# Two weight blocks split ahead of four projections, the ring's loads moved on SyncE's queue, squares added in pairs on GpSimd

## What is computed

```python
for i in range(4):
    h = adaln(x, norm_g[i, 0], shift[:, 0], scale[:, 0])
    x = x + 0.5 * gate[:, 0, None] * swiglu(h, ffn_w_in[i, 0], ffn_w_out[i, 0])
    h = adaln(x, norm_g[i, 1], shift[:, 1], scale[:, 1])
    y = (rwkv7_time_mix, mamba2_ssd_mix, swa_sink_attention)[i % 3](h, ...)
    x = x + gate[:, 1, None] * y
    h = adaln(x, norm_g[i, 2], shift[:, 2], scale[:, 2])
    x = x + 0.5 * gate[:, 2, None] * swiglu(h, ffn_w_in[i, 1], ffn_w_out[i, 1])
# rms_norm(x, g) = x * rsqrt(mean(x * x over features) + eps) * g
# adaln(x, g, shift, scale) = rms_norm(x, g) * (1 + scale) + shift
```

## Time and profile before

| | |
|---|---|
| Median of 3 runs | 3921.24 us (3918.16 to 3923.84) |
| The profiled execution's own time | 3914.14 us |
| Its span, first to last instruction | 3912.5 us |
| Busy: PE / DVE / ACT / POOL | 88% / 60% / 39% / 4% |
| Instructions on PE / DVE / ACT / POOL | 28885 / 3355 / 2038 / 148 |
| Mean granted TensorE clock | 0.905 |
| HBM read | 669 MB, 172 GB/s over the span |

### The profile page before, as it was taken

The page is one execution under the profiler, slowest core; times in us unless marked ns, Lnnn a source line. Parts: engine busy times, 40 slices in busy tenths (PEclk is TensorE's granted clock), DMA queues, the critical chain, the costliest instruction groups (busy, mean ns, idle before and its releaser), DMA issues. The chain is left out here.

```text
span 3912.5 us, 68263 instructions
## 1 busy us (share of the span) xinstructions
PE 3438.6 (88%) x28885; PEld 3248.8 (83%) x28885; DVE 2347.7 (60%) x3355; ACT 1507.4 (39%) x2038; POOL 155.0 (4%) x148
## 2 busy tenths in 40 slices
PE   6688999999985788999997499999599999859799
PEld 5578999999983778999995499999389998648599
DVE  5547886456764436767676557676657646354454
ACT  3314444434452114444462244444454444311243
POOL 0001111110000100000000000000000000001000
PEclk9769999998997888999996699999799999878799
DMA  8326885445831004768541047685037444200142
GB/s 338 130 119 245 314 311 228 182 187 225 313 135 54 2 2 180 299 235 310 213 172 46 1 186 297 231 310 202 35 153 297 188 185 159 77 21 2 75 175 84
DMA packets 74781, 676.76 MB, mean 173 GB/s; under 512 B 8480, under 2 KB 12608, under 8 KB 52160
## 3 DMA queue, kind: packets, MB, share of 16 engines
q1 hardware_dynamic: 30400, 509.96, 33.6%
q10 hardware_dynamic: 41472, 151.01, 10.1%
q0 software_dynamic: 2688, 12.59, 1.2%
HBM read 669.29 MB, written 4.23 MB: 172 GB/s over the span
## 5 line engine op out<-in xcount | busy, mean ns | idle before, releaser
L1109 DVE TENSOR_TENSOR w_split<-ring,w_split 128x1024 fp32r<-128x1024 f32 x705 | 873.5, 1242 | 603.5 <-ACT w_split L1004 601.1
L1004 ACT ACTIVATE w_split<-ring 128x1024 fp32r<-128x1024 f32 x705 | 742.8, 1057 | 1077.2 <-PE banks L934 853.5
L932 PE MATMUL banks<-u_split,w_split 128*128 128x256 f32 x3840 | 1093.1, 285 | 13.9 <-DVE w_split L1109 7.3
L933 PE MATMUL banks<-u_split,w_split 128*128 128x256 f32 x3840 | 1090.1, 284 | 0.0
L934 PE MATMUL banks<-u_split,w_split 128*128 128x256 f32 x3840 | 1089.9, 284 | 0.0
L932 PEld LDWEIGHTS banks<-u_split,w_split 128*128 128x128 f32 x3840 | 741.5, 193 | 19.8 <-DVE w_split L1109 16.2
L933 PEld LDWEIGHTS banks<-u_split,w_split 128*128 128x128 f32 x3840 | 741.2, 193 | 0.5
L934 PEld LDWEIGHTS banks<-u_split,w_split 128*128 128x128 f32 x3840 | 740.7, 193 | 0.0
L932 PE MATMUL banks<-h_split,w_split 128*128 128x256 f32 x1920 | 543.6, 283 | 2.9 <-DVE w_split L1109 2.9
L933 PE MATMUL banks<-h_split,w_split 128*128 128x256 f32 x1920 | 543.4, 283 | 0.0
L934 PE MATMUL banks<-h_split,w_split 128*128 128x256 f32 x1920 | 543.3, 283 | 0.0
(11 more groups left out here) (395 smaller groups left out, 3986.8 us busy)
## 6 DMA issues: line engine op xcount, KB each, us to landing
ring<-stream SPq DMA_DIRECT2D x147, 3072.0 KB, 10.8
bufs<-ada ACTq DMA_DIRECT2D x288, 512.0 KB, 10.9
bufs<-ada SPq DMA_DIRECT2D x8, 2048.0 KB, 9.0
bufs<-ada POOLq DMA_DIRECT2D x8, 1024.0 KB, 7.6
bufs<-c_rows SPq DMA_DIRECT2D x8, 512.0 KB, 4.3
bufs<-gate_rows POOLq DMA_DIRECT2D x32, 128.0 KB, 8.0
ring<-stream SPq DMA_DIRECT2D x3, 1024.0 KB, 4.9
ring<-stream SPq DMA_DIRECT2D x1, 2816.0 KB, 10.4
```

Source lines behind the costliest of these rows:

```text
L932: pe.matmul(out, w(0), x(0), start=start, stop=False, skip_group_check=True)
L933: pe.matmul(out, w(0), x(1), start=False, stop=False, skip_group_check=True)
L1004: nc.scalar.activation(w_split[:, slot, 0, :], piece(j, b), ACT.Copy).then_inc(high.sem, 1)
L1109: e = nc.vector.tensor_tensor(w_split[:, slot, 1, :], piece(j, b), w_split[:, slot, 0, :].bitcast(F32), ALU.subtract)
```

## The change

It has three parts.

1. *First blocks split ahead.* The first dense unit of each layer gets `ahead`: two keys (the first two blocks of the mixer's first projection, `r0`, `mb_in`, `sw_qk`, `r1`) and two slots. At its end ScalarE copies both high parts behind the unit's last ones, and VectorE writes the first low part ahead of the residuals and the second behind them. `core.split_early` is 2 in the next stage, so that `weight_high` and `weight_low` do nothing for those two blocks, and the waits count from there. The window projection takes its slots from buffer 8 in place of 7, and its band mask moves.
2. *Ring ahead of the stores.* In `first_ada_stage` unit 0 is issued ahead of the fourth ada slice, units 1 and 2 right behind it, and the two stores of bias rows come after them.
3. *Pairs.* `pair_sums` on GpSimd adds squares 2q and 2q+1; `token_sums` takes four chunks in place of eight. It is used in three centering stages, the norm behind the last of them, seven dense units and four output stages.

```diff
@@ first_ada_stage, SyncE
             for k in range(FIRST_HALVES):
                 if k >= 3:
+                    core.load_ahead(sync, None, 1)
                     sync.wait_ge(step.sem, step.at(4 * (k - 2)))
                 sync.dma_start(slots[k % 3], core.ada[k, :, :]).then_inc(loaded[k % 3].sem, loaded[k % 3].count(16))
+            core.load_ahead(sync, None, SLOTS - 1)
             for q in range(2):
                 sync.wait_ge(copied.sem, copied.at(4 * q + 4))
...
-            core.load_ahead(sync, None, SLOTS - 1)
             sync.wait_ge(stored.sem, stored.at(32))
@@ weight_high, weight_low (the first line), project_first_pair (the last two)
+    if b < core.split_early:
+        return
...
-    pe.wait_ge(low.sem, low.at(2))
+    if core.split_early < 2:
+        pe.wait_ge(low.sem, low.at(2))
@@ new
+def pair_sums(core, pool, squares, squared, paired, per=1, offset=0):
+
+    for q in range(KC // 2):
+        pool.wait_ge(squared.sem, squared.at((2 * q + 2) // per + offset))
+        pool.tensor_tensor(squares[:, 2 * q, :], squares[:, 2 * q, :], squares[:, 2 * q + 1, :], ALU.add)\
+            .then_inc(paired.sem, paired.count(1))
@@ NextNorm.on_tensor (center_stage alike)
-            token_sums(core, pe, self.squares, self.bank, self.squared, self.summed)
+            token_sums(core, pe, self.squares[:, 0:KC:2, :], self.bank, self.paired, self.summed, n=KC // 2)
@@ glu_stage, ScalarE
+            if ahead:
+                act.wait_ge(h_low.sem, h_low.at(n))
+                for key, slot in zip(*ahead):
+                    unit, at, size, _ = core.place[key]
+                    act.wait_ge(core.loaded[unit % SLOTS].sem, 16 * (unit // SLOTS + 1))
+                    act.activation(slot, core.ring[:, unit % SLOTS, at:at + size], ACT.Copy).then_inc(high.sem, 1)
+                high.made += len(ahead[0])
@@ glu_stage, VectorE
+            if ahead:
+                ahead_low(0)
             for c in range(KC):
...
+            if ahead:
+                ahead_low(1)
+                low.made += len(ahead[0])
             if after:
                 after.on_vector(dve)
@@ layer
-    layer_ffn(core, i, 0, early=2 if i else 0)
+    first = ("r0", "mb_in", "sw_qk", "r1")[i]
+    layer_ffn(core, i, 0, early=2 if i else 0, ahead=([(first, 0), (first, 1)], core.weight_slots(8)[0:2]))
```

More of the change, by code:

```diff
@@ L490, in project_split @@
     w = weight_parts(core, b, key, slots, kcs)
-    pe.wait_ge(low.sem, low.at(b + 1))
+    if b >= core.split_early:
+        pe.wait_ge(low.sem, low.at(b + 1 - core.split_early))
     for k in range(kcs):
@@ L797, in _ @@
                 root_of_tokens(core, act, turn=1)
+        @block.gpsimd
+        def _(pool):
+            pair_sums(core, pool, squares, squared, center_paired, per=2)
+            if after:
+                after.on_gpsimd(pool)
         @block.vector
@@ L845, in pair_norm_stage, with glu_stage @@
     core.end_stage()
-def glu_stage(core, key, n, src, residual, gates=None, ada=None, shift=None, early=0, pre=None, then=None, next_key=None):
+def glu_stage(core, key, n, src, residual, gates=None, ada=None, shift=None, early=0, pre=None, then=None, next_key=None, ahead=None):
     nc = core.nc
@@ L1101, in _ @@
                 gated.made += n
+        if gates is None and after:
+            @block.gpsimd
+            def _(pool):
+                after.on_gpsimd(pool)
         @block.vector
@@ L1201, in next_low, with ahead_low @@
                                         w_split[:, b, 0, :].bitcast(F32), ALU.subtract).then_inc(low.sem, 1)
+            def ahead_low(b):
+                key, slot = ahead[0][b], ahead[1][b]
+                unit, at, size, _ = core.place[key]
+                dve.wait_ge(high.sem, high.at(6 * n + b + 1))
+                nc.vector.tensor_tensor(core.ring_split[unit % SLOTS][:, at:at + size], core.ring[:, unit % SLOTS, at:at + size],
+                                        slot.bitcast(F32), ALU.subtract).then_inc(low.sem, 1)
             link = chain(core, dve, "dve")
@@ L1226, in glu_stage @@
     core.end_stage()
+    core.split_early = len(ahead[0]) if ahead else 0
 def log1p_series(dve, link, out, e, t, z):
```

23 lines of the change are left out of this document (16 added, 7 removed).

## The result

The changed kernel takes 3894.39 us against 3922.46 of the kernel before (medians of four runs each); the ratio is 0.9929, with a 95% interval of 0.9913 to 0.9945: 28 us or 0.7% less, 21.6 to 34 by the interval. One of the four, at 7354 us, was disturbed: it is left out of the ratio but counts in the median, which lies between 3888.38 and 3900.39. The forecast was 23.7 us less, 3897.5, and 3884 to 3913 for its range. The same kernel was timed twice more, with a ratio of 0.9924 (0.9908 to 0.9940) and one of 0.9945 (0.9930 to 0.9959), so the three give 21 to 30 us.

The account below looks back on a forecast made before the run. TensorE was busy for 88% of the span, so only seams between stages could shorten: 12.8 us (split blocks) + 16.5 (pairs) - 5.6 (load order) = 23.7 less than the median 3921.24, giving 3897.5 us; range 3884 to 3913.

Parts of the forecast that it names:

- The window wait: Window projection's start: TensorE no longer waits for a weight block's low part and starts 4.4 us earlier.
- The sign against it: Window stage: if the second product pair starts less than 3 us earlier, the split-block forecast is wrong.
- The byte count: Start, SyncE's queue: 11.5 MB take 26.8 us at 430 GB/s, then two stores of 2.1 MB take 4.9, until 60.9.
- a queue served in order: SyncE's queue at the start: stores issued behind the weight units land after them; next stage starts 13.6 us later.
- the rest of that stage keeps its distances: Stage after the stores: beyond the 7.99 us wait saved, nothing else shifts, so the net is 5.6 us lost.
- Rival A: Start: stores land beside the weight units, not held up; the load order gains 8.0 us, total 3883.9; chance 0.10.
- three centering stages: Sums in centering: TensorE's rows halve from 6.99 us, first add delays 0.7; gain 2.8 each, 8.4 in all.
- four output stages: Sums at output stages: tails shorten by 1.1 twice, 2.2 and 1.4 us, together 5.8.
- seven dense stages: Sums at dense units' ends: 0.6 us gained in each of three, 0.4 in all for the other four lost; 1.4 net.
- D: Projections: TensorE's earlier start does not carry through; split blocks gain only 0 to 3 us, total 3909; chance 0.09.
- B: Sums: pairs bring nothing, through the add's hand-over or GpSimd blocked by centering; total 3914.0; chance 0.13.
- C: Sums: a GpSimd add costs 1.57 us everywhere, so pairs lose 19 us, total 3933; chance 0.06.

Follow-up runs that it names:

- part 3 alone: Kernel before plus only the squares added in pairs on GpSimd, load order and block splits as before: 3903.01 us, ratio 0.9949 to the kernel before.
- part 1 alone: Kernel before plus only the two split blocks moved ahead, ring loads and sums as before: 3903.88 us, ratio 0.9958 to the kernel before.
- part 2 alone: Kernel before plus only the new load order on SyncE's queue at the start: 3924.01 us, ratio 1.0004 to the kernel before.

## Why the prediction was right, step by step

**Part 1** was right in its places and its size: 12.8 forecast, 16 (11 to 22) measured alone. The window wait fell by 4.40 (5.22 to 0.82), the Mamba wait by 4.40 (5.31 to 0.91), the wide ones by 2.05 and 2.06 (7.88 to 5.83, 7.77 to 5.71). These sum to 12.9. The sign against it, a second pair that starts less than 3 us earlier, did not come: it was 5.2. I had costed the moved subtractions at nothing; they cost 3.8 us, in part 3's tails, as shown above.

**Part 2** went the way that I forecast, against what the move might be thought to bring: the stage start at 62.29 for 62.5, the first product at 68.28 for 68.5. The byte count (11.5 MB at 430 GB/s, then 2.1) gave most of both, and two small errors cancelled: the second store landed at 61.7 and not at 60.9, and from there to the next stage's start it took 0.6 us and not 1.6. The net was 5.6 for a measured -1 to 4, from runs that can't exclude 5.6. What I had not reckoned with is that the shift may shrink on its way. The step "the rest of that stage keeps its distances" holds for the projection; the first output stage, where VectorE waits for its ada loads, gave back about half, and 2.8 us were left behind it on average. The reason was half right too: a queue served in order is what happens on SyncE's queue, but it is not needed for the loss, as the stores on their own queue show. Rival A (stores not held up) is out.

**Part 3** came to 16.5 in the forecast and 20 (13 to 27) alone. The tails, from the last square's end to the sums, say more than the total:

| places | forecast | before, sum of tails | after | gained |
|---|---|---|---|---|
| three centering stages | 8.4 | 16.0 | 8.2 | 7.8 |
| norm behind the last | 0.9 | 2.5 | 1.9 | 0.6 |
| four output stages | 5.8 | 11.8 | 6.6 | 5.2 |
| seven dense stages | 1.4 | 16.8 | 17.6 | -0.8 |

The sum is 12.8, inside the bounds of 6 and 21 but 3.7 under the forecast. In part 3 alone, where four of the dense stages have no subtraction, the tails sum to 31.0 us, 16.2 less than before. The term that was mis-sized is the dense one. I took 2.05 us for a dense tail, with the last add ending 1.4 behind the last square. It ends 1.7 behind, and the tail is 2.38 at the full clock and up to 2.79 below it. I had only let the add suffer from its neighbour, but the subtraction suffers as well (1.63 for 1.21). It starts at 1083.63, while the third add runs until 1084.18, and ends at 1085.26; the last add starts at 1084.24 and ends 0.58 us behind it, at 1085.84, which is less than the 0.73 that an add takes alone. That looks as if each had waited for the other in turn, though no run tests it. An add alone took 0.73 where I had 0.6.

**The chances.** D, B, C and A were each told apart by a run or a row and none happened. That the total came out 4 us from the forecast owes something to luck. The places touched account for 12.9 + 12.8 - 2.8 = 22.9 us, near the forecast's 23.7, because part 2 cost less and the dense stages gained less. The three timings gave 28, 30 and 21, each uncertain by some 6. What the first two have beyond the rows is not explained.

## What to carry over

Count bytes ahead of the transfer that ends a stage: a load moved into idle DMA time is free only up to that idle time and the slack that the last transfer has, and whatever is beyond it is paid by the stage's last transfer, on whichever queue that is. Put an added step where its engine is idle at that moment, not where the instruction is shortest, and read what stands beside it: here GpSimd's add and VectorE's subtraction of two SBUF tensors lengthened each other, while adds beside VectorE's residuals, which read one operand from PSUM, kept their 0.73 us. Check each of several edits by its own row in the trace, since a sum of three can be right for reasons that cancel.

## What the runs showed of the hardware

**Executions of one kernel differ by 12 us and more, and the granted clock with them.** Of fourteen executions of the changed kernel (all but the one at 7354 us), three have a mean granted clock of 0.907 and took 3900.4 to 3902.1 us; the eleven at 0.909 to 0.911 took 3887.2 to 3896.0. One place where it falls can be seen. The products of the RWKV state (weights of 32, 64 or 128 rows and 128 columns) are 128 in a run. Their sum in the changed kernel's first trace and its second:

```profile
L2089 PE MATMUL banks<-state,ring 64*128 64x256 f32 (+2 forms) x128 | 42.0, 465 | 2.8 <-ACT state L2107 2.8
```

```profile
L2089 PE MATMUL banks<-state,ring 64*128 64x256 f32 (+2 forms) x128 | 35.1, 406 | 2.8 <-ACT state L2107 2.8
```

Of fourteen traces, seven have 35.1 us there, the others 38.0 to 47.2, part 1 alone and part 2 alone the most. The stretch in the changed kernel's first trace, and the same work in the kernel before (the same 246 GB/s of DMA passes beside it):

```profile
3405.00:3410.00 5.00, 5.00 (x10) 2.24 (x10) 0.00 (x0) 0.60 (x1) 0.00 (x0) 0.50 0.57 246
```

```profile
3425.00:3430.00 5.00, 4.57 (x15) 2.06 (x14) 0.00 (x0) 1.18 (x3) 0.00 (x0) 1.00 0.57 246
```

TensorE is busy throughout, and its granted clock is nevertheless at the lower level (0.50, 1.2 GHz) in one and at 2.4 GHz in the other. Nearly all of the difference lies in one row, 32 products from 3399.44 on that take 16.14 us instead of 10.10. The level fell 2.8 us after they had begun, at 3402.2, and not during an idle stretch; the records don't show why in one execution and not in another.

This may be 6.9 of the profiled execution's 12 us (its siblings left no trace). It is not the only place. The second trace has 35.1 us here and yet the lower mean clock and 3902.1 us. Three stretches between sums, from the three traces of the changed kernel (us, mean granted clock):

| trace (span) | first RWKV layer's mixer | window mixer | second RWKV layer's mixer |
|---|---|---|---|
| first (3898.7) | 416.7, 0.810 | 177.9, 0.817 | 433.4, 0.799 |
| second (3900.4) | 419.4, 0.813 | 182.1, 0.789 | 427.8, 0.814 |
| third (3890.6) | 415.1, 0.822 | 177.0, 0.808 | 427.5, 0.818 |

Against the third, the first loses 5.9 us in the last stretch, the second 4.3 and 5.0 in the two others. So the place changes from one execution to the next. It is also why a single profile's span (3898.7 against 3912.5, 13.8 less) understated a gain of 28, and why edits worth under 5 us have to be judged at their rows.

**Two engines beside each other slow down both ways.** VectorE's subtraction of two SBUF tensors goes from 1.21 to 1.63 us beside GpSimd's adds, and an add from 0.73 to 1.61. I had expected only the second.

**Two full DMA queues moved equal numbers of packets, not of bytes.** With both full, from 44 to 50 us, GpSimd's queue moved 75 packets and SyncE's 81, but its packets were a third as large: it had 24% of the engines' time and SyncE's 77%, and the total stayed at 433 to 439 GB/s. Packets of equal size on both queues were not tried.
